# Modulation products placed one by one through a stage, and a gate's nonlinearity in one ScalarE activation, in a two-layer diffusion trunk on one core

## The reference, cut to what matters

```python
for l in range(2):                                  # DEPTH; h: 512 latent, 256 context tokens; D 1024, D_FF 2816
    m = split(silu(c) @ w_mod[l] + b_mod[l], 9)     # 9 vectors of 1024 for latents, 9 more for the context
    h = h + 0.5 * m[2] * swiglu(modulate(rms_norm(h, norm_ffn1[l]), m[0], m[1]), ffn1_w_gu[l], ffn1_w_down[l])
    u = modulate(rms_norm(h, norm_mix[l]), m[3], m[4]) @ w_in[l]
    ...                                             # four mixers: two attentions, a neighbourhood attention, a scan
    h = h + m[5] * (mix @ w_out[l])
    h = h + 0.5 * m[8] * swiglu(modulate(rms_norm(h, norm_ffn2[l]), m[6], m[7]), ffn2_w_gu[l], ffn2_w_down[l])

def swiglu(h, w_gu, w_down):
    gate, up = split(h @ w_gu, 2)
    return (silu(gate) * up) @ w_down
```

## Time and profile before

| | us |
|---|---|
| median of 3 runs (lowest, highest) | 3369.79 (3368.69, 3371.96) |
| profiled execution, its own time | 3370.19 |
| its span, first to last instruction | 3368.4 |
| TensorE busy in the span | 3153.7 |
| VectorE busy | 2325.9 |
| ScalarE busy | 1337.3 |

### The profile page before, as it was taken

One profiled execution on the slowest core, in us unless ns is written; L12 is line 12 of the kernel. 1 busy time (PEld: TensorE's weight loads), 2 busy tenths in 40 slices (PEclk: granted clock), 3 DMA queues, 4 the chain that ended last, 5 costly groups with the idle time before them and its releaser, 6 DMA issues. The chain is left out here.

```text
span 3368.4 us, 67001 instructions
## 1 busy us (share of the span) xinstructions
PE 3153.7 (94%) x27418; PEld 2794.3 (83%) x27418; DVE 2325.9 (69%) x3964; ACT 1337.3 (40%) x2382; POOL 405.3 (12%) x291
## 2 busy tenths in 40 slices
PE   6999999999989999999999999999999989899998
PEld 5898889886667878898888898998886668699897
DVE  5887778665667657878777987778655766555352
ACT  3343334325664333444324343343324654344231
POOL 2000000100706320000001000000100626120000
PEclk9999999999999999999999999999999999999999
DMA  5222322342000013222222322222242000123232
GB/s 204 94 76 88 94 88 76 127 157 88 2 18 3 16 50 100 63 94 76 94 88 70 105 71 94 84 87 86 88 156 90 2 18 4 40 82 102 85 87 94
DMA packets 70946, 264.44 MB, mean 79 GB/s; under 512 B 7840, under 2 KB 8992, under 8 KB 70048
## 3 DMA queue, kind: packets, MB, share of 16 engines
q1 hardware_dynamic: 70256, 256.95, 23.4%
q10 hardware_dynamic: 432, 3.88, 0.3%
HBM read 258.70 MB, written 2.10 MB: 77 GB/s over the span
## 5 line engine op out<-in xcount | busy, mean ns | idle before, releaser
L241 PE MATMUL ps<-hn_hi,w_hi 128*128 128x258 f32 (+1 forms) x1408 | 321.2, 310 | 12.2 <-PEq L955 8.1
L1049 ACT ACTIVATE pair_hi<-slot_sum 128x512 fp32r<-128x512 f32 x216 | 135.7, 630 | 477.2 <-DVE slot_sum L897 477.2
L241 PE MATMUL ps<-hn_hi,w_lo 128*128 128x258 f32 (+1 forms) x1408 | 319.3, 308 | 0.0
L241 PE MATMUL ps<-hn_lo,w_hi 128*128 128x258 f32 (+1 forms) x1408 | 318.6, 308 | 0.0
L218 ACT ACTIVATE w_hi<-raw 128x1024 fp32r<-128x1024 f32 (+1 forms) x119 | 131.3, 1103 | 446.7 <-PE ps L241 315.7
L1537 PE MATMUL ps<-m_lo,pair_hi 128*128 128x386 f32 x864 | 293.7, 340 | 0.0
L1537 PE MATMUL ps<-m_hi,pair_hi 128*128 128x386 f32 x864 | 293.0, 339 | 0.0
L223 DVE TENSOR_TENSOR w_lo<-raw,w_hi 128x1024 fp32r<-128x1024 f32 (+1 forms) x119 | 154.0, 1294 | 156.8 <-ACT w_hi L218 156.8
L241 PEld LDWEIGHTS ps<-hn_hi,w_hi 128*128 128x128 f32 x1408 | 222.4, 193 | 26.1 <-issue 11.7
L1016 POOL TENSOR_TENSOR out_sb<-out_sb,h_sq 128x768 f32<-128x768 f32 x18 | 35.9, 1994 | 1662.1 <-ACT h_sq L1201 1662.1
L241 PEld LDWEIGHTS ps<-hn_lo,w_hi 128*128 128x128 f32 x1408 | 221.4, 192 | 12.3
(11 more groups left out here) (390 smaller groups left out, 8013.6 us busy)
## 6 DMA issues: line engine op xcount, KB each, us to landing
raw<-wgu SPq DMA_DIRECT2D x176, 512.0 KB, 3.7
w_mod_one<-wmod SPq DMA_DIRECT2D x100, 512.0 KB, 3.6
raw<-wdn SPq DMA_DIRECT2D x66, 512.0 KB, 3.7
raw<-win SPq DMA_DIRECT2D x44, 512.0 KB, 4.6
w_mod_two<-wmod SPq DMA_DIRECT2D x28, 512.0 KB, 3.7
raw<-wdn_last SPq DMA_DIRECT2D x16, 704.0 KB, 4.0
w_mod_first<-wmod_first SPq DMA_DIRECT2D x4, 2048.0 KB, 23.1
raw<-wout SPq DMA_DIRECT2D x16, 512.0 KB, 3.6
```

What stands on the lines that cost most here:

```text
L241: mm = pe.matmul(out[:, o:o + b - a], w[:, k, :], m[:, k, a:b], start=(k == 0 and w is w_hi[s] and m is mov_hi), stop=(k == kt - 1 and w i ...
L1049: act.activation(flat(slot_hi[p]), quarter(3) if p == 6 else slot_sum[p][:, :], ACT.Copy).then_inc(slot_hi_ready.sem, 1)
```

## The change

The modulation products are placed anew: 0 to 5 in plain pairs 0 to 2, 6 in pair 3, 7 in the down pass of group 0 ahead of tile 0. In each of groups 1 to 4 one stands in the first pair, and in the down passes of groups 2, 3 and 4 there are four, behind tiles 0, 2, 4 and 6. SyncE's order there becomes: first modulation row, gate-side load, second row, up-side load, third and fourth row. In `gate_out` ScalarE writes twice the shifts into a small tile (a Copy of two columns, with a wait for it once per pair) and then silu(2y + 2 shift) in one activation per piece; VectorE's `silu` goes. The table set that holds Silu is loaded once per stage, ahead of the pairs of seven products. In the last group's down pass `gained_lo` of tile 6 goes ahead of `add_down` of tile 7.

```diff
+        shift_twice = at("shift_twice", [P, 2], R_W + WS + KD * P * 4)
...
             mods_of = {n: (2 * n, 2 * n + 1) for n in range(PLAIN)}
-            mods_of[FIRST[2] + 1] = (8,)
-            mods_of.update({("down", j): tuple(range(5 * j - 1, 5 * j + 4)) for j in (2, 3, 4)})
+            mods_of[PLAIN - 1] = (6,)
+            mods_of["down", 0] = (7,)
+            count = 8
+            for j in (1, 2, 3, 4):
+                mods_of[FIRST[j]] = (count,)
+                mods_of["down", j] = tuple(range(count + 1, count + (5 if j > 1 else 1)))
+                count += 1 + len(mods_of["down", j])
...
                             load(s, src)
-                            for m in mods[1:] if s == 0 else ():
+                            for m in mods[1:2] if s == 0 else mods[2:]:
                                 load_mod(m)
...
                         x = gate_s[:, C[half]]
+                        if half == 0:
+                            act.activation(shift_twice[:, :], gate_s[:, HT:HW], ACT.Copy, scale=2.0).then_inc(shift_ready.sem, 1)
+                            act.wait_ge(shift_ready.sem, shift_ready.at(n - PLAIN + 1))
                         for s, w in halves(half):
-                            act.activation(tanh_s[:, tokens(half, s)], x[:, s], ACT.Tanh, bias=shift_of(gate_s, w))
-                        for s, w in halves(half):
-                            mm = act.activation(gate_s[:, inner(half, s)], x[:, s], ACT.Identity, bias=shift_of(gate_s, w))
-                        mm.then_inc(tanh_ready.sem, 1)
+                            mm = act.activation(silu_s[:, tokens(half, s)], x[:, s], ACT.Silu, bias=shift_twice[:, w:w + 1], scale=2.0)
+                        mm.then_inc(silu_ready.sem, 1)
...
+                    act.preload_act_table_set("silu_and_others")
                     for j, z in enumerate(SIZES):
...
-                    def silu(n, half):
-                        dve.wait_ge(*half_of(tanh_ready, n, half))
-                        t = slice(half * HT, (half + 1) * HT)
-                        dve.scalar_tensor_tensor(out=tanh_s[:, t], in0=tanh_s[:, t], scalar=1.0, in1=gate_s[:, C[half]],
-                                                 op0=ALU.add, op1=ALU.mult).then_inc(silu_ready.sem, 1)
...
-                        for m in mods[:1]:
+                        for m in mods if j == 0 else ():
                             mod_product(m)
                         for t in range(KD):
+                            if j == LAST and t == 7:
+                                gained_lo(dve, 6, nxt[3], hn_hi_ready.at(KD + 1 + 8), nxt[4])
...
-                            for m in mods[1 + t:2 + t]:
+                            for m in mods[t // 2:t // 2 + 1] if j and t % 2 == 0 else ():
                                 mod_product(m)
...
-                            if j == LAST and t:
+                            if j == LAST and 0 < t < 7:
                                 gained_lo(dve, t - 1, nxt[3], hn_hi_ready.at(KD + 1 + t + 1), nxt[4])
...
                         mod_product(mods[0])
-                        if last_of(n):
-                            mod_product(mods[1])
                         scaled(n, 1)
...
                                 slot_lo_made(dve, 6, n + 1)
-                            silu(n, 0)
-                            silu(n, 1)
                             glu_out(n, 0)
```

More of the change, by code:

```diff
@@ L774, in build_trunk @@
         up_s = at("up_s", [P, 2 * 386], T0 + SLOT + 3104)
-        tanh_s = at("tanh_s", [P, NT], T0 + SLOT + 2 * 3104)
+        silu_s = at("silu_s", [P, NT], T0 + SLOT + 2 * 3104)
+        shift_twice = at("shift_twice", [P, 2], R_W + WS + KD * P * 4)
         base_s = at("base_s", [P, 386], R_W + KD * P * 4)
@@ L780, in build_trunk @@
         w_summed, combined, first_copied = sem("weight_sums"), sem("products_combined"), sem("first_product_copied")
+        shift_ready = sem("shift_doubled")
         product_done, tile_done = sem("product_done"), sem("down_tile_done")
@@ L839, in ffn_seven @@
             mods_of = {n: (2 * n, 2 * n + 1) for n in range(PLAIN)}
-            mods_of[FIRST[2] + 1] = (8,)
-            mods_of.update({("down", j): tuple(range(5 * j - 1, 5 * j + 4)) for j in (2, 3, 4)})
+            mods_of[PLAIN - 1] = (6,)
[5 more added lines that the diff above has]
+                count += 1 + len(mods_of["down", j])
             MODS = 24
+            assert count == MODS
             def order_of(n):
@@ L1269, in mod_product @@
                         for w in range(2):
-                            mm = dve.scalar_tensor_tensor(out=w_mod[0][:, :] if w else mod_waste[n >= 2 * PLAIN][:, :], in0=w_mod[0][:, :],
+                            mm = dve.scalar_tensor_tensor(out=w_mod[0][:, :] if w else mod_waste[n >= 2 * PLAIN - 1][:, :], in0=w_mod[0][:, :],
                                                           scalar=1.0, in1=cond_rows[:, w, :], op0=ALU.mult, op1=ALU.mult,
@@ L1315, in glu_out @@
                             mm = dve.scalar_tensor_tensor(out=up_s[:, inner(half, s)], in0=up_s[:, inner(half, s)],
-                                                          scalar=shift_of(up_s, w), in1=tanh_s[:, tokens(half, s)],
+                                                          scalar=shift_of(up_s, w), in1=silu_s[:, tokens(half, s)],
                                                           op0=ALU.add, op1=ALU.mult)
@@ L1586, in ffn_seven @@
             for x, n in ((x_own, len(OWN)), (m_hi_made, 15), (w_summed, 4 * SEVENS), (combined, 2 * PLAIN + 7 * SEVENS),
-                         (first_copied, SEVENS), (tanh_ready, HALVES), (silu_ready, HALVES), (glu_ready, HALVES),
+                         (first_copied, SEVENS), (tanh_ready, PLAIN), (shift_ready, SEVENS), (silu_ready, HALVES), (glu_ready, HALVES),
                          (g_hi_ready, HALVES), (g_lo_ready, HALVES), (slot_hi_ready, len(hi_at)), (slot_lo_ready, len(lo_at)),
```

## The result

The changed kernel takes 3249.32 us (median of 4 runs, 3248.60 to 3252.11) against 3370.54 us before: a ratio of 0.9642, interval 0.9625 to 0.9659. The forecast was 3264 us, range 3255 to 3290. So the kernel is 121 us faster, as forecast in kind, but 15 us more than forecast and 6 us outside the range.

The account below looks back on a forecast made before the run. TensorE, busy 94% of the span, was taken to bound the kernel. Gains of 85.5, 18.5 and 2.8 us (106.8) off 3370.2, less 0.4 for the median, plus 1 for small waits, gave 3264 us, range 3255 to 3290.

Parts of the forecast that it names:

- (a): Down passes of groups 2 to 4: four spread products replace five, the nine waits go; 85.5 us gained.
- Piece "7": Down passes of groups 2 to 4: piece TensorE's last tile needs, before 6.8 us late, now with 10 us to spare.
- product C: Down passes of groups 2 to 4: third of four modulation products, forecast to end 7 us ahead of the pass's end.
- The clock lost behind the waits: Behind the nine down-pass waits of groups 2 to 4: low granted clock costing 20 us, counted as regained.
- (b): Plain pair 3 keeps one product, the other moves to group 0's down pass; TensorE's second-tile wait goes; 18.5 us gained.
- R2: Rival: product moved into group 0's down pass delays add 0, tile 4 waits, 18.5 us come back: 3283 us; chance 0.07.
- (c): One product in the first pair of groups 1 to 4, none in pair 7; counted 0, at worst 1 us each.
- The ring in group 1: Group 1, two pairs alone: VectorE finishes pair 5's ring about when TensorE wants it; counted 0, at worst 1 us each.
- (d): Gate in the pairs: Silu replaces Tanh, Identity and VectorE's multiply; VectorE gains 1.03 us a pair, worth 0 to the sum.
- (e): Three more table loads, 1283 ns each, ahead of pair 4's first copy; counted 0, at most 4 us.
- R3: Rival: Silu's table set does not serve Copy, four reloads a pair, up to 277 us, 3541 us; chance 0.03.
- (f): Last group's down pass: gained_lo 6 ahead of add 7, so GpSimd sets the end; 0.95 x 3 = 2.8 us gained.

## Why the prediction was wrong in size

**(a) right.** 86.0 us against 85.5. The schedule worked out held, and all nine passes take 33.66 us (33.5 was the sign); with E = 291.61, the start of the next pair, VectorE's timeline has:

```profile
276.87 0.68 DVE L930 TENSOR_TENSOR slot_lo<-raw,slot_hi 128x512 fp32r<-128x512 f32 x1
...
282.56 1.23 DVE L1280 SCALAR_TENSOR_TENSOR mod_waste<-w_mod_one,cond_rows 128x1024 f32<-128x1024 f32 x1 [2.24 <-DMA w_mod_one<-wmod]
...
295.54 0.68 DVE L913 TENSOR_TENSOR slot_lo<-raw,slot_hi 128x512 fp32r<-128x512 f32 x1
```

Piece "7" is ready at E - 14.1 (forecast E - 14.3), product C ends at E - 6.8 (E - 7), the pass's last piece at E + 4.6 (E + 4.7). The clock lost behind the waits, 20 us of the sum, came back as counted.

**(b) right.** 18.9 us against 18.5; the moved product held nothing up (R2 did not come).

**(c) right with the gate, and by it alone.** The ring in group 1 waits 0.7 us in all. Without the gate it is 6.2 us, and 9.6 with the clock. The forecast had the two offset each other, and they do, though it priced the ring at no more than 1 us a stage even at worst, and the gate at 0. (A pair takes 15.7 us of VectorE by its numbers, not 15.8.)

**(d) is one of the two terms that failed.** "Neither bounds TensorE in a pair, so it is worth 0 to the sum" is true of the pairs and overlooks the last down pass, where VectorE stood on the path to the stage's end and was held up by GpSimd. There the gate alone took each wait from 4.1 us on average to 2.71, 4.1 us in all, and with the clock behind it about 6. The bounds on the new activation held: the Silu takes 620 ns where the Tanh took 614, the small Copy 193, as the groups of ScalarE show.

```profile
L1094 ACT ACTIVATE silu_s<-gate_s,shift_twice 128x384 f32<-128x384 f32 x54 | 33.5, 620 | 1.8
...
L1091 ACT ACTIVATE shift_twice<-gate_s 128x2 f32<-128x2 f32 x54 | 10.4, 193 | 7.7 <-DVE gate_s L1293 6.6
...
L1166 ACT ACT_TABLE_LOAD x3 | 3.8, 1283 | 0.1
```

**(e) right.** Three loads of 1283 ns more and no others; R3 did not come. The row agrees with the Trainium skill (ScalarE: Activation LUTs, Table sets): Copy and the Silu run in one set without a reload.

**(f) is the other.** "0.95 x 3 = 2.8 us" was nearly right for the wait (3.2 us on top of the gate), but the step took the rest of the stage end as unchanged: 0.9 us less idle time was its sign, and the three waits became 2.1, 2.4 and 2.8 us shorter. It had priced the clock behind the twelve waits inside the stage and not behind the three at its ends, where the same view has 0.72, 0.86 and 0.72 (608:620, 1837:1849, 2400:2412). With the wait at 1.66 us the clock stays at 1.00: 1.5 us more at each end than at 2.71. It also read GpSimd's end at 607.33 as a fixed floor. With the old gate GpSimd does set the end, but at 607.71, as it is held up by the pair that was moved ahead. With the new gate its last add, which waits for squares that follow VectorE's adds, starts 1.06 us ahead of the end of TensorE's pass, where it started 0.52 behind it, and the floor is gone.

Together: waits 7.3 and clock 6.7 us, 14.0 in place of 2.8. That is the 11 us that were missing, and the range had no case for it, since every unknown but one had been counted as a cost. (Its lower bound should read 3258: 3264 less 5 and less the 1 us for new waits.) The last 3 us are no more than two executions of the changed kernel differ by: 3.3 us ahead of the first down pass, and 1.6 between the first stage's end and the second's first down pass.

## What to carry to other kernels

When a kernel has one bounding engine and a price for its low clock, every wait of that engine is priced with the clock behind it, those at the ends of stages too; a microsecond off a wait of 3 to 4 us was worth about two here. Work taken off a second engine is worth nothing where it has slack, so look through all its passes for the one where it has none, and for what runs beside it there. A row's work with a single buffer has a fixed period (load plus use, 6.1 us here against tiles of 4.2): spread it over the tiles, and never put a piece that the bounding engine wants behind it.

## What the runs showed of the hardware

VectorE and GpSimd hold each other up. In the last down passes of the kernel before, ten of VectorE's instructions of L458 (scalar_tensor_tensor, two inputs in the on-chip memory) met an add of GpSimd that was under way or began with them. The six of 512 columns took 1.77 to 2.41 us, where 0.74 was usual, and the four of 256 columns 2.06 to 2.07, where 0.48 was. Each ended 0.55 us (512 columns) or 0.28 (256) after GpSimd's add did, whenever it had started, so it was held until then rather than slowed throughout. It goes the other way too: GpSimd's add of 768 columns mostly took 1.80 to 1.86 us, but twice 2.80, and ended there 1.70 us behind a pair of L458 that had started 0.04 us ahead of it. On average L458 took 1008 ns (512 columns) and 711 (256) in the kernel before, and 764 and 524 with GpSimd's adds made small. VectorE's add that reads TensorE's result memory took 1.14 us a pair with or without GpSimd beside it.

TensorE's granted clock behind a stage end, in windows of 12 us from the very restart, by the length of the wait ahead of it:

| wait, us | clock |
|---|---|
| 1.65 to 1.66 | 1.00 (twelve of twelve, in four executions) |
| 2.71 to 2.80 | 0.86 (eight of nine), 1.00 (one) |
| 3.06 to 3.50 | 0.86 to 0.88 (eight of nine), 0.75 (one) |
| 3.74 to 4.41 | 0.74 to 0.88 (nine) |

So a longer wait goes with a lower clock, but its length alone doesn't settle it. Inside the stage, behind the nine waits of 1.62 to 2.16 us in the kernel with the piece ahead of the product, the clock of the next 8 us was 1.00 five times and 0.79 or 0.80 four times, with no order by length (2.12 us kept 1.00, 1.74 did not). What decides between such waits stays open.
